# One mixture-of-experts layer: slot gates in the PSUM copy, and adding DMA loads onto the residual rows

## The chip, the core and the metric

The kernel runs on one core of one Trainium2 chip. The metric is the device time of one execution in microseconds (us). A profile of one execution gives the trace that is read here; its times count from the first instruction.

## What is computed

One layer of a streaming encoder over 512 tokens of width 1024, in float32. Two mixers (an SSD scan and an HGRN2 scan) and an output projection give the residual rows `x`. Behind them comes a mixture of 16 experts in 4 groups: each token takes its best group and in it the best two experts.

```python
p_group = jax.nn.softmax(t @ router_group);  g_idx = argmax(p_group);  g_w = max(p_group)
top_w, top_i = lax.top_k(jax.nn.softmax(in_group), 2)       # in_group: the group's 4 logits
top_w = top_w / jnp.sum(top_w)
combine = sum(one_hot(expert_id, 16) * (g_w * top_w))       # per token, 2 of 16 are not zero
hid = silu(t @ wg) * (t @ wu)                               # per expert, 256 wide
x = x + sum over experts of combine * (hid @ wd)
return rmsnorm(x, final_norm_w)
```

So each token ends as its residual row plus two expert rows, each times a gate, and then a norm.

## The kernel before

Every engine has its own instruction stream, written by hand; semaphores order them. The span has four parts: input projections and mixers (to about 255 us), output projection with the routers' logits (to 283), routing (283 to 298), experts (298 to 450), and a tail (450 to the end).

**Routing.** DVE turns the logits into one-hot choices and slots. `onehot` maps tokens to up to 112 slots of an expert. PE multiplies `onehot` with small tables (`find_all`, `find_targets`): `gix` says which token sits in a slot, `six` to which output row a slot's result goes. `keep_warm(n)` issues n matmuls whose result nobody reads. GpSimd (POOL) then gathers the token rows of experts 0 to 3 from `h2_dram` (L667), DVE works off the leftovers of routing (L1479 to L1494, the last of them counting rounds), splits expert weights into a high and a low part (`split_b` L1506, `split_c` L1512) and does the same to the gathered tokens (`rest_tokens` L1500) once PE has turned them (`turn_tokens` L1962) and ACT has copied them (L975). SP loads 3 MB of weights per expert, in the order in which splits free the buffers.

**Experts.** For each of 16 experts PE forms gate, up and down products, ACT copies the two halves of the output out of PSUM into `ysb` (L1008, L1010), and POOL scatters its 112 rows into `pairs_dram` (L688). That tensor has two halves of 512 rows: the row of the token's expert with the lower place in its group is in the first, the other's in the second. All rows of the first half are written once 12 of the 16 experts are done.

**Tail.** SP loads the first half in four loads of 0.5 MB (`load_early`, L544) after expert 13's work has been handed out, and DVE computes the gates (`gates`) and adds each loaded row times its gate to the residual row (L1570). SP loads the second half when all scatters have landed (L572). For each of four tiles of 128 tokens DVE adds (L1596), ACT sums squares and takes the root (L1036, L738), DVE norms (L1602), SP stores (L575).

**Later rounds.** If an expert has more than 112 tokens, everything from `find_all` on is repeated; each engine reads the number of rounds into a register (L443) and branches (L444) past the repeated code. With these inputs nothing is repeated. In the kernel before this stands ahead of the tail.

Of the kernel before, what the change touches and what calls it, by code (L numbers as in the profile page):

```python
# [5 lines left out]
ALU = mybir.AluOpType  # L6
# [37 lines left out]
def trunk(nc, x, norm_mix_w, w_units, w_dt, conv_w, conv_b, dt_bias, a_log, d_skip, ssd_norm_w, hgrn_lb_logits,  # L44
# [97 lines left out]
    with ExitStack() as ctx:  # L142
# [101 lines left out]
        onehot = gate[:, 0, :].bitcast(F16).rearrange("p (c t s) -> p c t s", c=2, t=TT)  # L244
        vals = part(TT * NE).bitcast(F16).rearrange("p (c t e) -> p c t e", c=2, t=TT)
# [11 lines left out]
        wcol = part(KD)  # L257
        rtw = part(KD * NL).rearrange("p (k n) -> p k n", k=KD)
        ss = part(TT * D // UC).rearrange("p (t u) -> p t u", t=TT)
# [13 lines left out]
        early = [raw[:, 1, 0:D], raw[:, 1, D:2 * D], arena[:, 0:D], arena[:, D:2 * D]]  # L273
        late = [arena[:, a:a + D] for a in range(8 * D, 12 * D, D)]
# [141 lines left out]
        res_ok = sem("res_ok")  # L416
# [9 lines left out]
        early_ok = sem("early_ok")  # L426
# [4 lines left out]
        h2_dram = nc.dram_tensor("h2_dram", (T, HROW), F32, kind="Internal").ap()  # L431
        pairs_dram = nc.dram_tensor("pairs_dram", (2 * T, D), F32, kind="Internal").ap()
# [7 lines left out]
        def later_rounds(eng, body):  # L440

            eng.wait_ge(routed, 1)
            n = eng.value_load(rounds[0:1, 0:1], min_val=1, max_val=MOST)  # L443
            with eng.If(n > 1):  # L444
                with eng.Fori(1, n) as r:
                    body(r, r * NE)
            return n
# [28 lines left out]
        def _(sp):  # L476
# [42 lines left out]
            def sp_round(r, base, first_round=False):  # L519
                for e in range(WSETS if first_round else 0, NE + 1):  # L520
# [9 lines left out]
                    if e < NE:  # L530
                        if e == 0:
                            sp.wait_ge(early_ok, r * TT)
                        else:
                            sp.wait_ge(wlb_ok, (base + max(e - WSETS + 1, 0)) * 2)
                        load_b(e)

            def load_early(rows_done, first_round=False):
                for j in range(YB):
                    sp.wait_ge(sca_out[j], rows_done)
                if first_round:  # L540
                    wait_a(sp, 0, NE - 2)
                    sp.wait_ge(wlb_ok, (NE - 2) * 2)
                for tt in range(TT):
                    sp.dma_start(early[tt], pairs_dram[tt * P:(tt + 1) * P, :]).then_inc(early_in, 16)  # L544

            def sp_later(r, base):
                sp_round(r, base)
                load_early(r * (16 * PER_Y) + 16 * PER_Y)
# [12 lines left out]
            load_c(2)  # L561
            sp.wait_ge(gat_in[0], 16)
# [4 lines left out]
            load_early((NE - G) // YB * 16, True)  # L567
            n = later_rounds(sp, sp_later)
            for j in range(YB):
# [3 lines left out]
            for tt in range(TT):  # L573
                sp.wait_ge(fin_ok, tt + 1)
                sp.dma_start(out[0, tt * P:(tt + 1) * P, :], late[tt]).then_inc(out_st, 16)  # L575
            sp.wait_ge(out_st, 16 * TT)

        @block.gpsimd
        def _(pool):
# [101 lines left out]
            def scatter(r, base, e):  # L681
# [3 lines left out]
                if e == 0:  # L685
                    pool.wait_ge(six_ok, r + 1)
# [3 lines left out]
                    .then_inc(sca_out[j], 16)  # L690

            def pool_round(r, base, first_round=False):
# [9 lines left out]
                for e in range(NE):  # L702
# [4 lines left out]
                    scatter(r, base, e)  # L707

# [5 lines left out]
            later_rounds(pool, pool_round)  # L714
# [10 lines left out]
        def _(act):  # L725
# [260 lines left out]
            def act_expert(r, base, e, first_round):  # L986
# [15 lines left out]
                if e + 2 < NE:  # L1002
                    round_b(r, e + 2)
                elif e + 1 < NE:
                    round_hidden(step + 1, e + 1)
                act.wait_ge(dn, step * 2 + 3)
                y_free(act, r, e, first_round)
                sc.activation(ysb[e % YB][:, 0:512], bank[5][:, :], ACT.Copy).then_inc(y0_ok, 1)  # L1008
                act.wait_ge(dn, step * 2 + 4)
                sc.activation(ysb[e % YB][:, 512:1024], bank[6][:, :], ACT.Copy).then_inc(y1_ok, 1)  # L1010
# [20 lines left out]
            later_rounds(act, act_round)  # L1031

            ch.link(sc.activation(dec[:, 0, 0:1], ident[:, 0:1], ACT.Sqrt))
            for tt in range(TT):
                act.wait_ge(res_ok, tt + 1)
                ch.link(sc.activation(X[:, tt, :], late[tt], ACT.Square, accum_out=st[:, 0, tt:tt + 1]))  # L1036
                root(st[:, 5, tt:tt + 1], st[:, 0, tt:tt + 1], 1.0 / D).then_inc(fsd_ok, 1)

        @block.vector
        def _(dve):  # L1040
# [427 lines left out]
            def targets(r):  # L1468

                dve.wait_ge(six_mm, r + 1)  # L1470
                ve.tensor_scalar(six, bank[7][:, NE:2 * NE], float(NO_SLOT), None, ALU.add).then_inc(six_ok, 1)
# [19 lines left out]
            for k in range(2, MOST):  # L1491
                ch.link(ve.scalar_tensor_tensor(rnd[:, 1:2], rnd[:, 0:1], float(k * CAP), rnd[:, 1:2], ALU.is_gt,
                                                ALU.add))
            ve.tensor_copy(rounds, rnd[:, 1:2]).then_inc(routed, 1)  # L1494
# [44 lines left out]
            def dve_round(r, base, first_round=False):  # L1539
# [543 lines left out]
```

## Time and profile before

| | us |
|---|---|
| median of 3 runs (lowest, highest) | 476.56 (475.51, 476.58) |
| the profiled execution, its own time | 476.44 |
| its span, first to last instruction | 474.7 |
| PE busy (share of the span) | 434.1 (91%) |
| DVE busy | 341.3 (72%) |
| ACT busy | 272.5 (57%) |
| POOL busy | 155.3 (33%) |

A view of the trace lists instructions with start, length, engine, source line, operation and, in brackets, how long the engine sat idle before and who released it. The chain of waits follows the work that ended last backwards. Engine time off that chain costs nothing. The timeline's length of a transfer issued by POOL is the time that POOL takes to issue it, not that of the data.

### The profile page before, as it was taken

To read this page: it belongs to the slowest core of one execution; us is meant where nothing else is said; L and a number is where in the kernel's file an instruction comes from. 1 tells how busy PE (TensorE), PEld (TensorE's weight loads), DVE (VectorE), ACT (ScalarE), POOL (GpSimd) and SP (SyncE) were. 2 spreads that over 40 slices of the span, in tenths; PEclk is the share of its full clock that TensorE was granted. 3 is DMA by queue.
4 is the path that set the end of the run, shared out by engine and by line. 5 is a ranking of instruction groups with operands and counts; after the bars stand their busy time and mean duration, and the time that the engine had idled before them with its cause. 6 is when DMAs were issued, how large, how long until landed. Compare 5 with 4: busy or idle time off the path is not lost.

```text
span 474.7 us, 7158 instructions
## 1 busy us (share of the span) xinstructions
PE 434.1 (91%) x2785; PEld 382.3 (81%) x2785; DVE 341.3 (72%) x523; ACT 272.5 (57%) x444; POOL 155.3 (33%) x114
## 2 busy tenths in 40 slices
PE   6999999999999899999999996999999999999800
PEld 4888888899998699899999986888888888887500
DVE  5535887783769689899866258677887787758836
ACT  6654182623543343228254335598998999879523
POOL 5620000000005000212400403388878887865210
PEclk9999999999999999999999998999999999999955
DMA  8632222222204002224199602989999999987264
GB/s 314 245 111 90 89 90 88 90 88 90 90 1 139 40 1 90 88 96 171 51 370 307 258 18 60 321 306 363 384 384 350 375 385 373 359 336 290 79 212 198
DMA packets 20626, 92.47 MB, mean 195 GB/s; under 512 B 4797, under 2 KB 7017, under 8 KB 12138
## 3 DMA queue, kind: packets, MB, share of 16 engines
q1 hardware_dynamic: 13848, 81.42, 45.9%
q0 software_dynamic: 4096, 8.41, 5.3%
q10 hardware_dynamic: 2642, 2.11, 1.4%
q8 instruction: 24, 0.39, 0.4%
q14 instruction: 16, 0.13, 0.1%
HBM read 86.69 MB, written 11.54 MB: 207 GB/s over the span
## 4 chain that ended last, share of the span: by engine, by line
PE 69%; DVE 14%; DMA 9%; ACT 6%; issue 2%; SPq 0%; POOLq 0%; DVEq 0%; ACTq 0%
PE bank L1641 41%; DMA arena<-in_w_gate_up_dram 5%; PE bank L1974 4%; PE bank L1976 4%; PE bank L1975 4%; PE bank L1962 2%; PE bank L1839 1%; DVE wl L1506 1%; DMA X<-in_x_dram 1%; DMA pairs_dram<-arena 1%; DVE actl L1052 1%; DVE actl L1512 1%; DMA X<-h_dram,arena 1%; PE bank L1711 1%; DVE arena L1602 1%
## 5 line engine op out<-in xcount | busy, mean ns | idle before, releaser
L1641 PE MATMUL bank<-wh,acth 128*128 128x256 f32 x320 | 91.8, 287 | 1.4 <-DVE actl L1052 0.8
L1641 PE MATMUL bank<-wl,acth 128*128 128x256 f32 x320 | 90.5, 283 | 0.0
L1641 PE MATMUL bank<-wh,actl 128*128 128x256 f32 x320 | 90.4, 283 | 0.0
L618 POOL TENSOR_TENSOR wl<-raw,wh 128x2048 fp32r<-128x2048 f32 x4 | 20.5, 5137 | 134.4 <-ACT wh L734 134.4
L1641 PEld LDWEIGHTS bank<-wh,acth 128*128 128x128 f32 x320 | 61.2, 191 | 1.8 <-issue 1.7
L1641 PEld LDWEIGHTS bank<-wl,acth 128*128 128x128 f32 x320 | 61.3, 192 | 0.0
L1641 PEld LDWEIGHTS bank<-wh,actl 128*128 128x128 f32 x320 | 61.2, 191 | 0.0
L1974 PE MATMUL bank<-wh,acth 128*128 128x512 f32 x128 | 51.7, 404 | 0.9 <-DVE wl L1506 0.7
L1976 PE MATMUL bank<-wh,actl 128*128 128x512 f32 x128 | 50.1, 392 | 0.0
L1975 PE MATMUL bank<-wl,acth 128*128 128x512 f32 x128 | 49.9, 390 | 0.0
L678 POOL TENSOR_TENSOR wl<-raw,wh 128x1024 fp32r<-128x1024 f32 x15 | 36.0, 2421 | 42.0 <-ACT wh L923 42.0
L1641 PE MATMUL bank<-acth,wh 128*128 128x512 f32 x112 | 44.1, 394 | 0.1
L1641 PE MATMUL bank<-acth,wl 128*128 128x512 f32 x112 | 43.6, 390 | 0.0
L1641 PE MATMUL bank<-actl,wh 128*128 128x512 f32 x112 | 43.6, 389 | 0.0
L678 POOL TENSOR_TENSOR wl<-arena,wh 128x1024 fp32r<-128x1024 f32 x16 | 39.0, 2463 | 13.0 <-ACT wh L923 13.0
L734 ACT ACTIVATE wh<-raw 128x2048 fp32r<-128x2048 f32 x18 | 34.4, 1909 | 15.4 <-PE bank L1641 15.4
L1512 DVE TENSOR_TENSOR actl<-arena,acth 128x1024 fp32r<-128x1024 f32 x30 | 35.9, 1234 | 1.3 <-ACT acth L937 1.0
L1058 DVE TENSOR_TENSOR wl<-raw,wh 128x2048 fp32r<-128x2048 f32 x14 | 32.0, 2288 | 3.5 <-ACT wh L734 3.4
L1500 DVE TENSOR_TENSOR actl<-bank,acth 128x512 fp32r<-128x512 f32 x32 | 20.6, 686 | 17.7 <-ACT acth L975 17.7
L1506 DVE TENSOR_TENSOR wl<-arena,wh 128x1024 fp32r<-128x1024 f32 x20 | 27.0, 1391 | 7.7 <-ACT wh L928 7.7
L937 ACT ACTIVATE acth<-arena 128x1024 fp32r<-128x1024 f32 x30 | 30.0, 1055 | 0.0
L1974 PEld LDWEIGHTS bank<-wh,acth 128*128 128x128 f32 x128 | 24.0, 188 | 6.7 <-issue 1.9
(349 smaller groups left out, 1016.8 us busy)
## 6 DMA issues: line engine op xcount, KB each, us to landing
raw<-in_w_units_dram SPq DMA_DIRECT2D x18, 1024.0 KB, 4.9
arena<-in_w_gate_up_dram SPq DMA_DIRECT2D x18, 1024.0 KB, 16.4
arena<-in_w_down_dram SPq DMA_DIRECT2D x16, 1024.0 KB
raw<-in_w_gate_up_dram SPq DMA_DIRECT2D x14, 1024.0 KB, 15.1
arena<-pairs_dram SPq DMA_DIRECT2D x6, 512.0 KB, 5.4
X<-in_x_dram SPq DMA_DIRECT2D x4, 512.0 KB, 5.2
arena<-in_x_dram SPq DMA_DIRECT2D x1, 2048.0 KB, 9.9
h_dram<-X ACTq DMA_DIRECT2D x4, 512.0 KB, 4.7
```

The costliest lines, as they stand in the source:

```text
L618: gp.tensor_tensor(wl[:, u % SPL, :], raw[:, u % RAW, :], wh[:, u % SPL, :].bitcast(F32), ALU.subtract).then_inc(wlp_ok, 1)
L678: gp.tensor_tensor(wl[:, 0, c], raw_a[b][:, c], wh[:, 0, c].bitcast(F32), ALU.subtract).then_inc(wla_ok, 1)
L734: sc.activation(wh[:, u % SPL, :], raw[:, u % RAW, :], ACT.Copy).then_inc(wh_ok, 1)
L937: sc.activation(down_high(e)[:, c], raw_c[e % WSETS][:, c], ACT.Copy).then_inc(whc_ok, 1)
L1058: ve.tensor_tensor(wl[:, u % SPL, :], raw[:, u % RAW, :], wh[:, u % SPL, :].bitcast(F32), ALU.subtract).then_inc(wl_ok, 1)
L1500: ve.tensor_tensor(gtl[b][:, c], bank[2 + h][:, :], gth[b][:, c].bitcast(F32), ALU.subtract).then_inc(gl_ok, 1)
L1506: ve.tensor_tensor(wl[:, 1, c], raw_b[e % WSETS][:, c], wh[:, 1, c].bitcast(F32), ALU.subtract).then_inc(wlb_ok, 1)
L1512: ve.tensor_tensor(down_low(e)[:, c], raw_c[e % WSETS][:, c], down_high(e)[:, c].bitcast(F32), ALU.subtract).then_inc(wlc_ok, 1)
L1641: ins = te.matmul(acc_ap, a, b, start=(j == 0), stop=(j == n - 1))
L1974: te.matmul(bank[b][:, :], ah, uh[:, k, :], start=(first and k == 0), stop=False)
L1975: te.matmul(bank[b][:, :], ah, ul[:, k, :], start=False, stop=False)
L1976: ins = te.matmul(bank[b][:, :], al_, uh[:, k, :], start=False, stop=(last and k == kh - 1))
```

## The change

1. **Gates move into routing.** The gates' arithmetic goes from behind the last expert to just behind `vals6`. A table of the gate values, as a sum of three bfloat16 parts (`gvp`), is multiplied with the same one-hot matrix on PE in 24 more small matmuls (`find_targets`), and gives `gsl`, one gate per slot and expert. The `keep_warm(4)` behind `find_targets` goes. Counting the rounds moves behind `split_c`, and `rest_tokens(0)` moves ahead of it.
2. **The gate is applied in the copy out of PSUM**, as the scale of the two ACT copies per expert.
3. **The additions are done by DMA.** `add_early` and `add_late`, issued by POOL, load rows of `pairs_dram` with `accum_op=add` onto the residual rows `xres`. DVE's eight additions of a tile and SP's eight loads go. `add_early` stands in POOL's stream behind the scatter of expert 13, `add_late` behind the last scatter; it waits until all scatters and the early additions have landed.
4. **The residual rows are kept** in `xres_dram` by two stores on SP (`keep_rows`, 1.5 and 0.5 MB), since later rounds would start again from them.
5. **The read of the number of rounds and the branch** come behind the tail: the tail is always done, and again if there were later rounds. On SP they stand behind the wait for the output stores.

```diff
+            def store_out(k):
+                for tt in range(TT):
+                    sp.wait_ge(fin_ok, k * TT + tt + 1)
+                    sp.dma_start(out[0, tt * P:(tt + 1) * P, :], xres[:, tt, :]).then_inc(out_st, 16)
+                sp.wait_ge(out_st, (k + 1) * 16 * TT)
...
+            sp.wait_ge(ev_dve, evacuated(n_in_groups + halves_out.index((n_front - 2, 1)))[1])
+            keep_rows(slice(0, units[n_front - 1][1]))
+            sp.wait_ge(h2_st, 16 * (n_front - n_in + 1))
+            keep_rows(slice(units[n_front - 1][1], D))
             sp.wait_ge(gat_in[0], 16)
             load_a(3)
...
-            load_early((NE - G) // YB * 16, True)
-            n = later_rounds(sp, sp_later)
-            for j in range(YB):
-                sp.wait_ge(sca_out[j], n * (16 * PER_Y))
-            for tt in range(TT):
-                sp.dma_start(late[tt], pairs_dram[T + tt * P:T + (tt + 1) * P, :]).then_inc(late_in[tt], 16)
...
+            store_out(0)
+            later_rounds(sp, sp_round, rows_again, lambda n: store_out(1))
...
+            def add_early(k):
+                pool.sem_inc(pool_tick, 1)
+                for tt in range(TT):
+                    gp.dma_start(xres[:, tt, :], pairs_dram[tt * P:(tt + 1) * P, :],
+                                 accum_op=ALU.add).then_inc(early_in, 16)
+
+            def add_late(k):
+                pool.wait_ge(early_in, (k + 1) * 16 * TT)
+                pool.sem_inc(pool_tick, 1)
+                for tt in range(TT):
+                    gp.dma_start(xres[:, tt, :], pairs_dram[T + tt * P:T + (tt + 1) * P, :],
+                                 accum_op=ALU.add).then_inc(late_in[tt], 16)
...
+                weight = gsl[:, PERM[e]:PERM[e] + 1]
+                sc.activation(ysb[e % YB][:, 0:512], bank[5][:, :], ACT.Copy, scale=weight).then_inc(y0_ok, 1)
...
+            gv = r16[:, 4:6]
+            ch.link(ve.tensor_tensor(gv, r16[:, 1:3], r1[:, 8:10].unsqueeze(3).broadcast_to([P, 2, TT, NE]), ALU.mult))
+            for i in range(2):
+                ch.link(ve.tensor_copy(gvp[:, i], gv))
+                ch.link(ve.tensor_tensor(gv, gv, gvp[:, i], ALU.subtract))
+            ve.tensor_copy(gvp[:, 2], gv).then_inc(gt_v, 1)
...
                 split_b(base, 0, 0)
                 split_b(base, 0, 1)
+                rest_tokens(base, 0)
                 split_c(base, 0, 0)
-                rest_tokens(base, 0)
                 split_c(base, 0, 1)
+                if first_round:
+                    count_rounds()
...
+                pe.wait_ge(gt_v, 1)
+                for c in range(2):
+                    for tt in range(TT):
+                        for i in range(3):
+                            ins = te.matmul(bank[7][:, 2 * NE:3 * NE], onehot_b[:, c, tt, :], gvp[:, i, c, tt],
...
                 keep_warm(8)
                 find_targets(r)
-                keep_warm(4)
                 turn_tokens(r, base, 0)
```

DVE at the end of routing, where `CAST arena<-arena 128x128` makes a part of the gate table. Before:

```order
L1488 TENSOR_TENSOR arena<-arena 128x64 x2
L1492 SCALAR_TENSOR_TENSOR arena<-arena 128x1 x3
L1494 CAST arena<-arena 128x1
L1506 TENSOR_TENSOR wl<-raw,wh 128x1024 x2
L1512 TENSOR_TENSOR actl<-arena,acth 128x1024
L1500 TENSOR_TENSOR actl<-bank,acth 128x512 x2
L1512 TENSOR_TENSOR actl<-arena,acth 128x1024
```

and in the changed kernel:

```order
L1522 TENSOR_TENSOR arena<-arena 128x64 x2
L1526 TENSOR_REDUCE arena<-arena 128x4
L1528 SCALAR_TENSOR_TENSOR arena<-arena 128x4
L1529 RECIPROCAL arena<-arena 128x4
L1530 TENSOR_TENSOR arena<-arena 128x4
L1533 TENSOR_TENSOR arena<-arena 128x128
L1535 CAST arena<-arena 128x128
L1536 TENSOR_TENSOR arena<-arena 128x128
L1535 CAST arena<-arena 128x128
L1536 TENSOR_TENSOR arena<-arena 128x128
L1537 CAST arena<-arena 128x128
L1555 TENSOR_TENSOR wl<-raw,wh 128x1024 x2
```

Ten operations come ahead of the first weight split, four leave that place; `rest_tokens` (L1549 in the changed kernel) follows the split at once.

POOL from the scatter of expert 13 to the branch. Before:

```order
L678 TENSOR_TENSOR wl<-arena,wh 128x1024 x2
L688 DMA pairs_dram<-arena 1024x1024 x3
L443 TENSOR_LOAD arena
L443 ISA x2
L444 COMPARE_AND_BRANCH
```

and in the changed kernel:

```order
L677 TENSOR_TENSOR wl<-arena,wh 128x1024 x2
L687 DMA pairs_dram<-arena 1024x1024
L694 DMA arena<-pairs_dram 128x1024 x4
L687 DMA pairs_dram<-arena 1024x1024 x2
L701 DMA arena<-pairs_dram 128x1024 x4
L447 TENSOR_LOAD arena
```

Four loads stand between the scatters of experts 13 and 14, four behind that of expert 15.

SP behind its last weight load. Before:

```order
L566 DMA bc<-in_final_norm_w_dram 128x1024
L544 DMA raw<-pairs_dram 128x1024 x2
L544 DMA arena<-pairs_dram 128x1024 x2
L443 TENSOR_LOAD arena
L443 ISA x2
L444 COMPARE_AND_BRANCH
```

and in the changed kernel:

```order
L573 DMA bc<-in_final_norm_w_dram 128x1024
L547 DMA out_dram<-arena 128x1024 x4
L447 TENSOR_LOAD arena
L447 ISA x2
L448 COMPARE_AND_BRANCH
```

The eight loads of `pairs_dram` are gone from SP, and the value load with its branch stands behind the output stores.

## Rows read from the trace of the kernel before

**Rows 1.** The chain that ended last, from 449 us: start, length, what.

```profile
449.93 0.61 ACT arena L1010
...
451.38 5.36 DMA pairs_dram<-arena
...
456.82 3.51 DMA arena<-pairs_dram
```

**Rows 2.** The timeline of the tail: start, length, engine, line, operation [idle before].

```profile
451.38 1.35 POOL L688 DMA_INDIRECT pairs_dram<-arena  x1 [1.04 <-ACT arena L1010]
...
460.45 2.48 DVE L1596 SCALAR_TENSOR_TENSOR arena<-arena,raw 128x1024 f32<-128x1024 f32 x2 [7.34 <-DMA arena<-pairs_dram]
...
468.65 1.06 ACT L1036 ACTIVATE X<-arena 128x1024 f32<-128x1024 f32 x1 [1.11 <-DVE arena L1596]
...
470.17 0.16 DVE L1601 RECIPROCAL st<-st 128x1 f32<-128x1 f32 x1 [0.15 <-ACT st L738]
470.36 1.28 DVE L1602 SCALAR_TENSOR_TENSOR arena<-arena,st,bc 128x1024 f32<-128x1024 f32 x1
```

**Rows 3.** Source line L142, the end of the block.

```profile
L142 SPq COMPARE_BRANCH  x1: 38/38/38, 474.3 to 474.3; - x1
```

**Rows 4.** Transfers on pairs_dram from 420 us to the end.

```profile
L572 SPq DMA_DIRECT2D arena<-pairs_dram x4: 323/424/432, 456.8 to 458.1; - x4
...
DMA to landing us min/median/max: 3.5/5.4/7.2
```

**Rows 5.** A window of 2 us in the late loads; last columns DMA share, GB/s.

```profile
460.00:462.00 2.00, 0.00 (x0) 0.00 (x0) 1.54 (x2) 0.16 (x1) 0.00 (x0) 0.50 0.99 383
```

**Rows 6.** The timeline of POOL from 425 us.

```profile
430.58 0.96 POOL L688 DMA_INDIRECT pairs_dram<-arena  x1 [3.93 <-ACT arena L1010]
...
438.83 1.91 POOL L688 DMA_INDIRECT pairs_dram<-arena  x1 [1.12 <-ACT arena L1010]
448.58 1.76 POOL L688 DMA_INDIRECT pairs_dram<-arena  x1 [7.84 <-ACT arena L1010]
```

**Rows 7.** The timeline of POOL at the first gathers.

```profile
291.55 1.23 POOL L667 DMA_INDIRECT X<-h_dram,arena  x1 [4.30 <-DVE arena L1466]
293.08 1.87 POOL L667 DMA_INDIRECT X<-h_dram,arena  x1 [0.31 <-issue]
```

**Rows 8.** Source line L443, the value load ahead of the later rounds.

```profile
L443 SPq TENSOR_LOAD <-arena x1: 478/478/478, 430.1 to 430.1; - x1
```

**Rows 9.** Source line L444, the branch past the later rounds.

```profile
L444 DVEq COMPARE_BRANCH  x1: 72/72/72, 449.2 to 449.2; - x1
```

**Rows 10.** Source line L570, what SP does behind its branch.

```profile
L570 SPq ALU_OP  x1: 48/48/48, 431.1 to 431.1; - x1
```

**Rows 11.** Source line L1591, what DVE does behind its branch.

```profile
L1591 DVEq ALU_OP  x1: 57/57/57, 452.0 to 452.0; - x1
```

**Rows 12.** The timeline of DVE at the end of routing.

```profile
288.31 0.29 DVE L1454 TENSOR_REDUCE arena<-arena 128x8 f32<-128x128 f32 x1
...
291.89 0.54 DVE L1492 SCALAR_TENSOR_TENSOR arena<-arena 128x1 f32<-128x1 f32 x3
...
292.86 2.36 DVE L1506 TENSOR_TENSOR wl<-raw,wh 128x1024 fp32r<-128x1024 f32 x2 [0.24 <-issue]
...
297.16 1.29 DVE L1500 TENSOR_TENSOR actl<-bank,acth 128x512 fp32r<-128x512 f32 x2 [0.81 <-ACT acth L975]
```

**Rows 13.** The timeline of PE at the end of routing.

```profile
293.06 0.35 PE L1952 MATMUL bank<-arena,gate 128*128 128x16 f16 x8
...
295.84 1.09 PE L1962 MATMUL bank<-ident,X 128*128 128x128 f32 x8 [1.43 <-DMA X<-h_dram,arena]
```

**Rows 14.** Windows around the expert stage; last columns PEclk, DMA share, GB/s.

```profile
340.00:380.00 40.00, 40.00 (x197) 33.41 (x197) 31.88 (x35) 36.67 (x53) 32.79 (x18) 1.00 0.99 373
436.00:448.00 12.00, 10.73 (x48) 8.10 (x47) 10.73 (x18) 7.98 (x13) 3.62 (x2) 1.00 0.33 130
270.00:278.00 8.00, 8.00 (x70) 7.99 (x69) 2.90 (x6) 1.84 (x7) 2.11 (x1) 1.00 0.01 3
```

More of the change, by code:

```diff
@@ L257, in trunk @@
         wcol = part(KD)
+        gvp0 = ofs[0]
         rtw = part(KD * NL).rearrange("p (k n) -> p k n", k=KD)
+        part(3 * TT * NE - KD * NL)
+        gvp = arena[:, gvp0:gvp0 + 3 * TT * NE].bitcast(BF16).rearrange("p (i c t e) -> p i c t e", i=3, c=2, t=TT)
+        gsl = part(NE)
         ss = part(TT * D // UC).rearrange("p (t u) -> p t u", t=TT)
@@ L271, in trunk @@
         rounds = part(1).bitcast(I32)
-        early = [raw[:, 1, 0:D], raw[:, 1, D:2 * D], arena[:, 0:D], arena[:, D:2 * D]]
-        late = [arena[:, a:a + D] for a in range(8 * D, 12 * D, D)]
         assert ofs[0] <= 22528
@@ L438, in trunk, with later_rounds @@
         PER_Y = NE // YB
-        def later_rounds(eng, body):
+        def later_rounds(eng, body, before=None, after=None):
             eng.wait_ge(routed, 1)
@@ L444, in later_rounds @@
             with eng.If(n > 1):
+                if before is not None:
+                    before()
                 with eng.Fori(1, n) as r:
                     body(r, r * NE)
-            return n
+                if after is not None:
+                    after(n)
         def set_uses(r, e, sets):
@@ L690, in scatter, with add_again @@
                     .then_inc(sca_out[j], 16)
+            def add_early(k):
[9 more added lines that the diff above has]
+                                 accum_op=ALU.add).then_inc(late_in[tt], 16)
+            def add_again(n):
+                for j in range(YB):
+                    pool.wait_ge(sca_out[j], n * (16 * PER_Y))
+                pool.wait_ge(xres_in, 32)
+                add_early(1)
+                add_late(1)
             def pool_round(r, base, first_round=False):
@@ L707, in pool_round @@
                     scatter(r, base, e)
+                    if first_round and e == NE - 3:
+                        for j in range(YB):
+                            pool.wait_ge(sca_out[j], (NE - G) // YB * 16)
+                        pool.wait_ge(xr_st, 32)
+                        add_early(0)
             split_a(0, 0)
@@ L713, in _ @@
             pool_round(0, 0, True)
-            later_rounds(pool, pool_round)
+            for j in range(YB):
+                pool.wait_ge(sca_out[j], 16 * PER_Y)
+            add_late(0)
+            later_rounds(pool, pool_round, None, add_again)
         def conv_at(jj):
@@ L1030, in _, with final_sums @@
             act_round(0, 0, True)
[L1031 to L1037, printed above, removed]
+            def final_sums(k):
+                ch.link(sc.activation(dec[:, 0, 0:1], ident[:, 0:1], ACT.Sqrt))
+                for tt in range(TT):
+                    act.wait_ge(late_in[tt], (k + 1) * 16)
+                    ch.link(sc.activation(X[:, tt, :], xres[:, tt, :], ACT.Square, accum_out=st[:, 0, tt:tt + 1]))
+                    root(st[:, 5, tt:tt + 1], st[:, 0, tt:tt + 1], 1.0 / D).then_inc(fsd_ok, 1)
+            final_sums(0)
+            later_rounds(act, act_round, None, lambda n: final_sums(1))
         @block.vector
```

101 lines of the change are left out of this document (37 added, 64 removed).

## The prediction

> **What bounds the kernel now.** I read the chain of waits first, then the timeline of its last 25 us, then the places that the change touches. Up to 450 us the chain is PE and the weights' DMA, and in the expert stage the DMA engines are as good as full: a share of 0.99 at 373 GB/s from 340 to 380 us [rows 14]. Behind the last PSUM copy, which ends at 449.93 + 0.61 = 450.54, everything is a chain of handovers [rows 1]: the last scatter from its issue at 451.38 to its landing 5.36 us later (456.74), the first late load 3.51 us (456.82 to 460.33), and then tile work. That work is paced by DVE, which has an addition and a norm of 1.28 us for each tile, and its last norm ends at 470.36 + 1.28 = 471.64 [rows 2]. The last store has landed when SP goes on at 474.3 [rows 3]. So 24 of the 474.7 us are tail, and most of the change is there.
>
> **The tail, step by step, in times of this trace.**
>
> 1. *Last scatter.* Its issue took POOL 1.35 us [rows 2], and one took 0.96 us where DVE was less in the way [rows 6]. In the changed kernel DVE has no additions there, so I take 0.96: it lands 0.39 earlier, at 456.35. The start, 0.84 us behind the copy's end (450.54 to 451.38), stays.
>
> 2. *POOL answers instead of SP.* SP issued 0.08 us after the landing (456.74 to 456.82); POOL needs 0.84 as above. First adding load: issue at 456.35 + 0.84 = 457.19.
>
> 3. *First adding load, if it were a plain one.* On SP: 3.51 us from issue, of which 0.32 are SP's own issue (the shortest of four) [rows 4], so 3.19 behind it. On POOL with 0.96 of issue: 457.19 + 0.96 + 3.19 = 461.34.
>
> 4. *Pace.* Plain loads of 0.5 MB ran at 383 GB/s with the engines at a share of 0.99 [rows 5], which makes 1.37 us for each. An adding load has to fetch the old row as well as the new one before it can write. The trace of before has no such load. From below it costs what a plain one does, 1.37; the other end is two transfers' worth, 2.74, since engines at 0.99 have no time left for a second fetch. I take 2.74 for this reason. Then the first lands at 461.34 + 1.37 = 462.71 and the fourth 3 x 2.74 = 8.22 later, at 470.93. POOL's issues (four of about 1.3 us with their gaps) are faster than that.
>
> The Trainium skill, "Collectives: The Full Stack", in the section "The bandwidth ceiling: the fold count and why AG ≠ RS ≠ AR", says that a transfer which reduces runs at about half the speed of a copy because it reads two sources, not because the addition takes time. It speaks of collectives and no run here shows it yet; by it the pace is the 2.74 of step 4, and without it the sum would be that of the first rival. It is the rule that speaks most against this change.
>
> 5. *From the fourth landing to the end.* DVE began 0.12 after a landing (460.33 to 460.45); ACT now takes its place. From the start of the last square (468.65) to the end of the last norm (471.64) are 2.99, and from there to the landed store at 474.3 are 2.66 [rows 2, 3]. 470.93 + 0.12 + 2.99 + 2.66 = 476.70. DVE's addition is gone here, but at this pace it would have been hidden for all tiles except the last.
>
> 6. *Value load and branch on SP* stood at 430 us behind the early loads, under a long wait; now they stand behind the wait for the stores, where nothing covers them. From the value load at 430.1 to SP's next instruction behind the branch at 431.1 is 1.0 us [rows 8, 10]. 477.7, and the end of the block another 0.4 (474.3 to 474.7 as before): 478.1, so +3.4 against the span of 474.7. On the other engines the same pieces lie under the stores: DVE's takes 0.9 + 2.8 us from its load on, but it starts as soon as the last norm is issued.
>
> 7. *Early adding loads ahead of the last scatters.* POOL is free at 438.83 + 1.91 = 440.74 [rows 6] and starts 0.3 later. Its issue beside busy DVE costs up to 1.9 each [rows 7], so four end by 449.9 at the latest, against 448.58, when the scatter of expert 14 is issued; with 0.96 at its best they end at 446. That is covered within about 1 us. The data is the larger matter: first landing at 441.05 + 0.96 + 3.19 + 1.37 = 446.6, the fourth at 454.8, its data moved some 1.8 earlier (3.19 - 1.37), at 453.0. The two last scatters are issued by the same engine into the same queue; if they line up behind, their 2 x 0.46 MB need at least 2 x 1.2 us at 383 GB/s and 1.8 to land: 457.2, or 458 if they don't run at full speed, against 456.35. I take +1.4. Bounds: 0 (they pass by) to 3.
>
> Sum: +3.4 + 1.4 = +4.8, against the profiled execution's own 476.44 (span 474.7 and 1.7 around it): **481.2**. The median of the runs shown, 476.56, is 0.1 from it, so nothing is shifted.
>
> **What costs nothing, and its cover.** *DVE in routing:* behind the target table (at about 291.9) come four operations on 4 elements, some 0.2 each, and six on 128 elements, 0.29 for the like [rows 12] and 0.03 between: 0.8 + 1.9 = 2.7, to 294.6, where 1.0 stood before. The split starts at 294.6 instead of 292.86, takes 2.36 and ends at 297.0; the next on the path, `rest_tokens`, started at 297.16 because it waited for ACT [rows 12], and that waited for the gathered rows. So the cover is 0.2 us; it holds only because `split_c` moves behind. What is late next is SP's second and third load (1 us later), behind a first one of 1 MB, which at 373 GB/s [rows 14] is 2.8 us of data. *PE:* 24 matmuls at 0.35 for 8 [rows 13] are 1.05, from 294.6 to 295.7, and the turning of the first gathered rows behind them began at 295.84: cover 0.1 us. If both covers fail, routing slips by 0.3 to 1 us, of which the full DMA engines of the expert stage take back a part. *Keeping the rows:* 1.5 MB go where the DMA share is 0.01 (270 to 278) [rows 14], 0.5 MB behind the last store of token rows and ahead of the gathers, whose first is issued at 291.55 [rows 7]. *Scale in the PSUM copy:* same instruction, none added; ACT's new wait for the gate table stands before its first such copy, which needs all products of expert 0 first. *Gates, early additions and early loads* taken away: DVE sat idle for 7.34 us before the first late addition [rows 2], and the DMA share behind 436 was 0.33 [rows 14]. Nothing gained.
>
> **The rivals.**
>
> *A, on the other side: the adding loads run like plain ones.* Then the fourth lands at 461.34 + 3 x 1.37 = 465.45, and DVE, with a norm and a reciprocal for each tile (0.16 + 1.28 and gaps, 1.48) instead of an addition more, sets the end: the first norm starts at 461.34 + 0.12 + 1.71 = 463.17 (468.65 to 470.36 is the 1.71), the last ends 3 x 1.48 + 1.28 later at 468.9, store 2.66, SP 1.0, end 0.4: 473.0, so -1.7 and **474.7**. For it: the engines may fetch from SBUF beside DRAM. Against it: their share of 0.99. It decides at 4x = 7.56, a pace x of 1.9 us for each 0.5 MB: slower than that is a loss.
>
> *B, nothing to measure.* As A, but SP's branch costs what DVE's does, which is 2.8 us from the branch at 449.2 to the next instruction at 452.0 [rows 9, 11], not 0.1: +1.8 on A, **476.5**. Or a pace near 1.9. Against it: SP's own branch over nearly the same code was short. The Trainium skill, "Runtime: NRT & Kernel Launch", section "Instruction fetch mechanics", says that a taken branch to code outside the loaded window stalls for a fetch; by that rule SP's tail would be 2.8 longer whenever its code has moved across such a border, and the two rows here show both cases.
>
> *C, much slower.* If an adding load's fetch, fetch and write follow one another for each row, the pace is 3 x 1.37 = 4.11: fourth landing at 464.1 + 12.3 = 476.4, +8.9, and the early loads hold the last scatters back by some 7 us: **492**. Nothing in the trace speaks for or against it but that the operation is new.
>
> **How the numbers follow.** The forecast 0.55, A 0.22, B 0.12, C 0.11. A measurement of this kernel can tell some 0.3% (1.4 us) from no change. A is faster with nearly all its chance, B is same, forecast and C are slower: 0.23, 0.13, 0.64. The forecast's own range is 478.5 (no scatter held back, pace 2.4) to 484 (scatters 3 late, routing 1 late). For 8 in 10 I reach down to A and up to a pace of about 3: 474.5 to 486, which leaves out C and the edge of A.
>
> **What the next profile would show.** Right: loads issued by POOL behind the last scatter, landing 2.5 to 3 us apart; ACT's squares waiting for each of them; about 1 us between SP's last wait and the end. Wrong: squares or norms back to back with no wait for a landing (A); a gap of 3 us behind SP's branch (B); scatters of experts 14 and 15 that land as before in spite of slow early loads (step 7); `rest_tokens` later than 297.2, or the granted clock down behind 293 (routing).

## The result, and the profile after

The changed kernel takes 480.73 us (median of 4, 479.93 to 484.35), the kernel before beside it 476.46 (4 runs, 475.51 to 476.58). The ratio is 1.0112 with an interval of 1.0068 to 1.0156: slower, by 0.7 to 1.6%. The profiled execution took 479.94, its span is 478.2.

I read the chain of waits first, as for before. From the end of the last PSUM copy on it shows start, length, what:

```profile
449.23 0.70 ACT arena L1040
...
450.79 6.01 DMA pairs_dram<-arena
...
457.37 1.71 POOL arena L701 x2
459.07 11.71 DMA arena<-pairs_dram
470.79 0.02 issue
470.81 1.16 ACT X L1066 x2
...
472.52 1.28 DVE arena L1627
```

The last copy ends at 449.92, 0.6 earlier than before [rows 1], and the last scatter lands at 456.80, where it landed at 456.74: up to here nothing is lost. Then one piece of 11.71 us stands where 3.51 stood [rows 1]: the last adding load. The timeline of the same stretch shows who waits for it:

```profile
457.37 3.67 POOL L701 DMA_DIRECT2D arena<-pairs_dram  x4 [5.60 <-DMA pairs_dram<-arena]
463.07 1.06 ACT L1066 ACTIVATE X<-arena 128x1024 f32<-128x1024 f32 x1 [11.65 <-DMA arena<-pairs_dram]
...
465.51 1.06 ACT L1066 ACTIVATE X<-arena 128x1024 f32<-128x1024 f32 x1 [0.96 <-DMA arena<-pairs_dram]
...
467.99 1.06 ACT L1066 ACTIVATE X<-arena 128x1024 f32<-128x1024 f32 x1 [1.00 <-DMA arena<-pairs_dram]
...
470.81 1.06 ACT L1066 ACTIVATE X<-arena 128x1024 f32<-128x1024 f32 x1 [1.34 <-DMA arena<-pairs_dram]
```

Each of the four squares has an idle time ahead of it that a load ended, so the DMA sets the pace, where DVE did before [rows 2]. The landings (462.99, 465.49, 467.97, 470.79) are 2.60 us apart on average. The windows show the engines full, and the data at a little over half its rate (last columns DMA share, GB/s):

```profile
444.00:452.00 8.00, 5.05 (x22) 3.41 (x20) 0.92 (x3) 4.51 (x7) 1.99 (x2) 1.00 1.07 208
462.00:470.00 8.00, 0.00 (x0) 0.00 (x0) 3.37 (x6) 4.33 (x9) 0.00 (x0) 0.50 1.06 215
```

The first line is the early adding loads (with packets of the last two scatters among them), the second the late ones; plain loads had 383 GB/s at 0.99 [rows 5]. The end of the program, by source line, is SP's value load behind the wait for the stores and the branch behind it, whose rows had stood at 430 and 431 [rows 8, 10]:

```profile
L447 SPq TENSOR_LOAD <-arena x1: 462/462/462, 477.0 to 477.0; - x1
```

```profile
L448 SPq COMPARE_BRANCH  x1: 45/45/45, 477.8 to 477.8; - x1
```

The stores have landed at 476.98 and the span ends at 478.20. Routing, in the timeline of DVE (first fence) and PE (second), to be held against [rows 12, 13]:

```profile
294.65 0.23 DVE L1537 CAST arena<-arena 128x128 bf16<-128x128 f32 x1
295.04 2.39 DVE L1555 TENSOR_TENSOR wl<-raw,wh 128x1024 fp32r<-128x1024 f32 x2 [0.16 <-issue]
298.57 1.29 DVE L1549 TENSOR_TENSOR actl<-bank,acth 128x512 fp32r<-128x512 f32 x2 [1.15 <-ACT acth L1002]
```

```profile
294.94 0.76 PE L1980 MATMUL bank<-arena,gate 128*128 128x16 bf16 x24 [2.08 <-DVE arena L1537]
296.34 1.66 PE L1991 MATMUL bank<-ident,X 128*128 128x128 f32 x8 [0.64 <-issue]
...
299.35 0.77 PE L2003 MATMUL bank<-wh,acth 128*128 128x512 f32 x1
```

PE stands idle for 2.08 us until the gate table is there, and turns the tokens at 296.34 instead of 295.84; `rest_tokens` starts 1.41 later than before, and still waits for ACT.

**How tails are compared.** When the last PSUM copy ends varies by some 2 us each way between executions (449.9 to 454.2 in the profiles of this study). What follows it doesn't vary so: "the tail" below is the time from the end of that copy to the end of the span. Two profiles of one kernel on two chips gave 23.49 and 23.48 (the last experiment); single terms inside a tail differ more than that. Before it is 474.68 - 450.53 = 24.2, after it 478.20 - 449.92 = 28.3. So the tail lost 4.1 us, and the measured ratio stands for 0.0112 x 476.46 = 5.3 us (3.2 to 7.4); the medians differ by 4.3.

### The profile page after: what moved, and what is told of

The parts are those of the page before. It is cut to its first block, busy times and chain, and to the rows that moved or that the text cites. A ratio compares the mean times of both kernels' runs of the same rounds, so it can differ in the third digit from the quotient of the medians.

```text
span 478.2 us, 7184 instructions
## 1 busy us (share of the span) xinstructions
PE 434.9 (91%) x2801; PEld 383.8 (80%) x2801; DVE 333.6 (70%) x516; ACT 275.7 (58%) x444; POOL 159.5 (33%) x122
## 4 chain that ended last, share of the span: by engine, by line
PE 77%; DVE 11%; DMA 5%; ACT 5%; issue 1%; POOL 0%; SPq 0%; POOLq 0%; DVEq 0%
PE bank L1663 43%; PE bank L2003 6%; PE bank L2005 6%; PE bank L2004 6%; PE bank L1991 3%; DMA arena<-pairs_dram 2%; PE bank L1861 1%; DMA pairs_dram<-arena 1%; DMA X<-in_x_dram 1%; DVE actl L1085 1%; PE bank L1733 1%; PE bank L1734 1%; PE bank L1741 1%; PE bank L2028 1%; ACT arena L781 1%
## 5 line engine op out<-in xcount | busy, mean ns | idle before, releaser
L1663 PEld LDWEIGHTS bank<-wh,acth 128*128 128x128 f32 x320 | 61.3, 192 | 1.2 <-issue 1.0
L1663 PEld LDWEIGHTS bank<-wh,actl 128*128 128x128 f32 x320 | 61.3, 191 | 0.0
L1549 DVE TENSOR_TENSOR actl<-bank,acth 128x512 fp32r<-128x512 f32 x32 | 20.6, 686 | 16.8 <-ACT acth L1002 16.8
L1555 DVE TENSOR_TENSOR wl<-arena,wh 128x1024 fp32r<-128x1024 f32 x20 | 28.8, 1480 | 4.2 <-ACT wh L955 4.2
L2005 PEld LDWEIGHTS bank<-wh,actl 128*128 128x128 f32 x128 | 24.1, 188 | 5.3
```

The costliest lines, as they stand in the source:

```text
L1549: ve.tensor_tensor(gtl[b][:, c], bank[2 + h][:, :], gth[b][:, c].bitcast(F32), ALU.subtract).then_inc(gl_ok, 1)
L1555: ve.tensor_tensor(wl[:, 1, c], raw_b[e % WSETS][:, c], wh[:, 1, c].bitcast(F32), ALU.subtract).then_inc(wlb_ok, 1)
L1663: ins = te.matmul(acc_ap, a, b, start=(j == 0), stop=(j == n - 1))
L2005: ins = te.matmul(bank[b][:, :], al_, uh[:, k, :], start=False, stop=(last and k == kh - 1))
```

## The experiments

The theory was the prediction's: the tail is longer because an adding load costs the DMA engines two transfers, the branch adds 1 us, the early adding loads hold the last scatters back, and the move of the gates costs nothing. The rivals were that the loss lies in routing, that it comes from how POOL issues such a load, or from its rows.

**Gates in routing alone.** The kernel before with part 1 and 2 of the change: SP loads, DVE adds (now without a gate), the branch is ahead of the tail.

```diff
-                    ve.scalar_tensor_tensor(early[tt], early[tt], r1[:, 10, tt:tt + 1], xres[:, tt, :], ALU.mult,
-                                            ALU.add).then_inc(early_ok, 1)
+                    ve.tensor_tensor(early[tt], early[tt], xres[:, tt, :], ALU.add).then_inc(early_ok, 1)
```

> The kernel before with the gates made in routing and applied in the PSUM copies, but with SP's plain loads and DVE's additions as before (now without a factor), no stored residual rows and the branch ahead of the tail. Theory (the adding loads are the loss): no change against before, 476.5 within 1 us, since the routing slip of about 1.4 us in the changed kernel was gone again at the end of the experts. Rival (the routing slip reaches the end): 478, and the last PSUM copy ends 1 us or more later than at 450.5.

Measured: 476.14 (12 runs, 474.28 to 479.03), ratio 1.0003 (0.9978 to 1.0028), tail 23.5. Half of the change costs nothing and gains nothing that can be measured, though its profiled tail is 0.7 shorter than before's 24.2, and though routing is late in this kernel too: from the first gather to the first product of the experts it takes 298.68 - 290.87 = 7.8 us, before 297.91 - 291.55 = 6.4.

**Late loads plain.** The changed kernel with the four late loads on POOL, where they were, but without the addition. It leaves out what `xres` held, the residual and the first rows.

```diff
-                    gp.dma_start(xres[:, tt, :], pairs_dram[T + tt * P:T + (tt + 1) * P, :],
-                                 accum_op=ALU.add).then_inc(late_in[tt], 16)
+                    gp.dma_start(xres[:, tt, :],
+                                 pairs_dram[T + tt * P:T + (tt + 1) * P, :]).then_inc(late_in[tt], 16)
```

> The changed kernel with the four late loads plain instead of adding, still issued by POOL; this leaves the other expert's row and the residual row out of the result. Theory (two fetches for each adding load): the landings stand 1.3 to 1.5 us apart instead of 2.5 to 2.8, DVE's norms set the end, and the time falls by about 5 us, to 475. Rival (the software queue or POOL's issue sets the pace, not the addition): landings stay 2.5 apart and the time stays at 480.

Measured: 476.98 (12 runs, 474.65 to 480.02), ratio 1.0018 (0.9990 to 1.0046), tail 24.2: 4.1 less than with the addition, which is as much as the tail had lost. The chain of waits of this kernel:

```profile
454.06 6.07 DMA pairs_dram<-arena
...
460.70 1.11 POOL arena L701 x2
461.81 6.54 DMA arena<-pairs_dram
468.35 0.02 issue
468.37 1.16 ACT X L1066 x2
```

The landings are 464.32, 465.63, 468.35 and 469.61, so 1.31, 2.72 and 1.26 apart. The third came 1.4 late. Stores of finished tiles are not the reason: the first was issued at 467.49, and without the delay the third load would have landed at 466.9. The kernel before shows the same step: its plain loads landed at 460.33, 461.61, 464.07 and 465.34, and its first store was issued at 464.86. The windows around its third landing (last columns DMA share, GB/s):

```profile
463.00:464.00 1.00, 0.00 (x0) 0.00 (x0) 0.61 (x2) 0.98 (x2) 0.00 (x0) 0.50 0.40 160
464.00:465.00 1.00, 0.00 (x0) 0.00 (x0) 1.00 (x2) 0.65 (x3) 0.00 (x0) 0.50 0.06 25
```

A share of 0.06 is one engine of 16. The trace has 16 reports of each load, one from each engine, and the landing is the last of them. Of that third load 15 reports came from 462.39 to 462.90 and the last at 464.07: one engine was 1.2 us late. In the kernel with plain late loads it was several (12 reports by 467.05, the others from 467.64 to 468.35). Why is open. So plain loads of 0.5 MB land 1.67 us apart on average in the kernel before, and 1.76 here, though most engines keep a pace of about 1.3.

**Two adding, two plain.** The first two late loads add, the other two don't. It leaves out the residual and first rows of tiles 2 and 3.

```diff
-                for tt in range(TT):
+                for tt in range(2):
                     gp.dma_start(xres[:, tt, :], pairs_dram[T + tt * P:T + (tt + 1) * P, :],
                                  accum_op=ALU.add).then_inc(late_in[tt], 16)
+                for tt in range(2, TT):
+                    gp.dma_start(xres[:, tt, :],
+                                 pairs_dram[T + tt * P:T + (tt + 1) * P, :]).then_inc(late_in[tt], 16)
```

> The changed kernel with late adding loads for the first two tiles and plain ones for the last two; this leaves the other summands out of tiles 2 and 3. Theory: two landings about 2.6 apart and two about 1.3 to 2, so the fourth landing comes 1.5 to 2.5 us earlier than in the changed kernel counted from the first issue (13.4 there), and the tail from the last PSUM copy to the end shrinks by as much, from 28.3 to about 26. Rival (a fixed price for using adding loads at all): no earlier than with four.

Measured: 479.81 (12 runs, 477.95 to 481.61), ratio 1.0073 (1.0043 to 1.0104), tail 26.1, in the middle between 24.2 and 28.3. Landings 465.98, 468.52, 469.80, 471.07: 2.54 apart for the second adding load, 1.28 and 1.27 for the plain ones. One kernel, one queue, one execution, and the windows in each half (last columns DMA share, GB/s):

```profile
463.00:468.00 5.00, 0.00 (x0) 0.00 (x0) 0.32 (x2) 1.44 (x3) 0.35 (x1) 0.50 1.05 208
469.00:471.00 2.00, 0.00 (x0) 0.00 (x0) 1.04 (x3) 1.97 (x5) 0.00 (x0) 0.50 1.03 420
```

The engines are full in both; in the first the adding loads move 208 GB/s, in the second the plain ones 420 (stores of finished tiles counted).

**Short rows.** The late adding loads of a tile in two halves of 512 columns, so with rows of 2 KB.

```diff
-                    gp.dma_start(xres[:, tt, :], pairs_dram[T + tt * P:T + (tt + 1) * P, :],
-                                 accum_op=ALU.add).then_inc(late_in[tt], 16)
+                    for c in (slice(0, D // 2), slice(D // 2, D)):
+                        gp.dma_start(xres[:, tt, c], pairs_dram[T + tt * P:T + (tt + 1) * P, c],
+                                     accum_op=ALU.add).then_inc(late_in[tt], 16)
```

> The changed kernel with each late adding load cut into two of 512 columns, so rows of 2 KB instead of 4 KB, same bytes. Theory (each byte is fetched twice): a tile still lands every 2.5 to 2.8 us, its packets take half as long as the 4 KB ones (about 150 ns instead of 300), time within 1 us of the changed kernel's. Rival (each row pays a fetch, add and write in turn, whatever its length): twice the rows, so a tile every 4 to 5 us and 485 to 490.

Measured: 484.20 (4 runs, 482.01 to 485.78), ratio 1.0160 (1.0092 to 1.0228), tail 30.8. The squares of the four tiles:

```profile
465.66 1.06 ACT L1067 ACTIVATE X<-arena 128x1024 f32<-128x1024 f32 x1 [11.92 <-DMA arena<-pairs_dram]
...
469.15 1.06 ACT L1067 ACTIVATE X<-arena 128x1024 f32<-128x1024 f32 x1 [2.01 <-DMA arena<-pairs_dram]
...
471.82 1.06 ACT L1067 ACTIVATE X<-arena 128x1024 f32<-128x1024 f32 x1 [1.20 <-DMA arena<-pairs_dram]
...
475.73 1.06 ACT L1067 ACTIVATE X<-arena 128x1024 f32<-128x1024 f32 x1 [2.43 <-DMA arena<-pairs_dram]
```

3.38 us for each 0.5 MB. Neither side's number came out. The records of single packets tell more: the median adding packet of 2 KB took 178 ns, one of 4 KB in the changed kernel 328, a plain one of 4 KB in the kernel with plain late loads 159. So an adding packet costs by its bytes, at 4 KB twice a plain one, with about 28 ns beside that (2 x 178 - 328, an estimate from the two sizes). Of 0.5 MB each of the 16 engines moves 8 packets of 4 KB: 8 x 328 ns = 2.62 us, the pace seen with adding loads, and 8 x 159 = 1.27, which is the pace of plain ones where no engine is late. With 2 KB it is 16 x 178 = 2.85. The other 0.5 us of the 3.38 have a likely source in the queue rows. Here the stores of finished tiles (q1) run among the late loads, from 465.57 to 475.71:

```profile
q0 software_dynamic: 783, 1.41, 80.9%
q1 hardware_dynamic: 264, 1.00, 24.7%
```

That is 2.5 us of every engine. In the changed kernel, between its first and fourth landing, the same queue took 13.2% of 7.80 us, so 1.0. The difference is 1.5 us for three spacings, or 0.5 for each, as much as was missing. It was not tested by itself.

**No early adding loads.** It leaves out the first expert rows.

```diff
-                        add_early(0)
...
-                pool.wait_ge(early_in, (k + 1) * 16 * TT)
```

> The changed kernel without the four early adding loads; this leaves the first expert's rows out of the result. Prediction's step 7: the last scatter's data lined up behind them, so its landing, 6.01 us behind its issue, comes back to 5.4 or less and the time falls by 0.5 to 1.4 us. Rival: the landing stays and so does the time.

Measured: 481.68 (4 runs, 479.10 to 483.36), ratio 1.0102 (1.0049 to 1.0154), tail 27.4, 0.9 shorter than after. The time doesn't show it: 0.9 us is 0.2% and lies inside the interval of 4 runs. The chain of waits does:

```profile
455.40 4.16 DMA pairs_dram<-arena
```

The last scatter needs 4.16 us from issue to landing, and 6.01 behind early adding loads; in the five other profiles with such loads it needed 5.79 to 6.15. Against the kernel before, where it took 5.36, the loss is smaller: 0.65. Of the 1.85 some 0.3 each are lost again ahead of the scatter, until the fourth landing and behind it.

**No later rounds.** The value load and the branch are taken away on all engines (these inputs need one round).

```diff
-            later_rounds(sp, sp_round, rows_again, lambda n: store_out(1))
```

> The changed kernel without the reading of the number of rounds, the branch and the repeated code on all engines; this leaves out later rounds, of which these inputs need none. Theory: SP's value load and branch lie bare behind the stores, so the time falls by 1.0 us, to about 479. Rival (a fetch behind the branch): by 2.8 us. Other rival (hidden): by nothing.

Measured: 480.53 (4 runs, 478.58 to 482.06), ratio 1.0101 (1.0047 to 1.0155), tail 26.6, 1.7 shorter than after. The end of the block on SP:

```profile
L142 SPq COMPARE_BRANCH  x1: 33/33/33, 477.2 to 477.2; - x1
```

The span ends at 477.58, 0.4 behind the landed stores; after it ends 1.2 behind them. So 0.8 us are the value load and the branch on SP. The other 0.9 of the shorter tail lie ahead of that: the last scatter lands 0.2 sooner, the four loads take 0.1 less, and the last store lands 2.65 us behind the last norm instead of 3.18. The first two are no more than what a single term varies by. The third is not chance. In all six profiled kernels whose branch stands behind the tail this store took 3.0 to 3.6 us from its issue, and in the six others, this one among them, 2.6. In the six with the longer store ACT and DVE branch 0.2 to 1.1 us before it is issued, in the changed kernel ahead of 473.83:

```profile
L448 ACTq COMPARE_BRANCH  x1: 50/50/50, 473.2 to 473.2; - x1
L448 DVEq COMPARE_BRANCH  x1: 72/72/72, 473.5 to 473.5; - x1
```

Behind these, from 473 to the end of the span, the instruction queue (q14) uses the DMA engines, which it does in none of the six others:

```profile
q14 instruction: 4, 0.03, 2.4%
```

Its four packets of 8 KB hold an engine for 0.3 to 0.6 us each, and of the changed kernel's last store 15 parts were reported by 476.54, the last at 476.98. That the loading of code is what holds that part back is argued, not tested. With it the branch's new place costs about 1.3 us instead of 0.8. The times don't show any of this: by the ratios this kernel is 0.5 us faster than the changed one, inside the noise.

**Warm matmuls back.** `keep_warm(4)` between the product of the targets and the wait for the gate table.

```diff
+                keep_warm(4)
                 pe.wait_ge(gt_v, 1)
```

> The changed kernel with the four warming matmuls put back, between the target product and the wait for the gate table. Theory of routing: TensorE's granted clock no longer falls to half around 296 us, and the first gate and up product starts about 1 us earlier than at 299.4; the time falls by 0 to 1 us, since the full DMA engines of the expert stage decide. Rival (the slip goes through): by the whole 1 to 1.4 us.

Measured: 480.98 (6 runs, 479.58 to 483.01), ratio 1.0106 (1.0053 to 1.0158), tail 28.4. In the changed kernel the granted clock is at its lower level, 1.2 of 2.4 GHz, for 3.4 us from 296.7, with PE idle for 2.08 us shortly before; here that drop is missing (one of 3.4 us stands at 289.7) and the turning takes 1.09 us again:

```profile
297.17 1.09 PE L1992 MATMUL bank<-ident,X 128*128 128x128 f32 x8 [1.04 <-DMA X<-h_dram,arena]
```

But it waits for the gathered rows, and the experts start no earlier: 299.74, 7.3 us behind the first gather, as in the changed kernel. Nothing is gained: the clock was not what made routing late. That the drop is missing needn't be the work of the four matmuls either: it is missing in the next experiment too, which doesn't have them.

**POOL adds the last tile.** The kernel of the first experiment, with the last late addition on POOL.

```diff
+            pool.wait_ge(res_ok, 1)
+            pool.wait_ge(late_in[TT - 1], 16)
+            gp.tensor_tensor(late[TT - 1], late[TT - 1], early[TT - 1], ALU.add).then_inc(res3_ok, 1)
```

> The kernel of the first experiment (gates applied in the PSUM copies, plain loads) with the last tile's addition done by POOL instead of DVE. DVE sets the end of the tail there with an addition and a norm of 1.28 us for each tile, POOL adds in about 2.5 us what landed at 465.9: theory, the tail from the last PSUM copy shrinks by 0.3 to 1.0 us from 23.5, the time by as much, too little to be sure of. Rival (the two engines hold each other up): longer.

Measured: 476.54 (12 runs, 474.73 to 478.12), ratio 1.0008 (0.9978 to 1.0037), tail 23.7. The timeline of DVE, and that of POOL:

```profile
466.45 3.18 DVE L1615 SCALAR_TENSOR_TENSOR arena<-arena,st,bc 128x1024 f32<-128x1024 f32 x1
```

```profile
465.48 3.06 POOL L724 TENSOR_TENSOR arena<-arena 128x1024 f32<-128x1024 f32 x1 [11.88 <-DMA arena<-pairs_dram]
```

A norm that takes 1.28 alone takes 3.18 beside POOL's addition: it gives back what DVE was spared.

**One adding load.** The same kernel with the last tile's late rows added by one adding load, where DVE might hide it.

```diff
-            for tt in range(TT):
+            for tt in range(TT - 1):
                 sp.dma_start(late[tt], pairs_dram[T + tt * P:T + (tt + 1) * P, :]).then_inc(late_in[tt], 16)
...
+            gp.dma_start(early[TT - 1], pairs_dram[2 * T - P:2 * T, :],
+                         accum_op=ALU.add).then_inc(late_in[TT - 1], 16)
```

> The kernel of e1 (gates in routing, plain loads by SP, additions by DVE), but the last of the four late tiles is added by one adding load that POOL issues; DVE adds three tiles and norms four. POOL's two waits ahead of it are written for one round, which is what these inputs need. Theory (an adding load costs two transfers' worth of the DMA engines and nothing else, so one of them is hidden where DVE sets the pace): the engines have 3 x 1.3 + 2.6 = 6.5 us of late data, the last landing is about 9 us behind the last scatter's, and in e1 DVE began its last addition 10 us behind it. So the adding load is hidden, DVE has one operation of 1.22 us less, and the tail from the end of the last PSUM copy to the end of the span is 22.4 us where e1 had 23.5; the ratio to before is 0.998, within 0.3% of no change. Rival (the adding load takes its share from the plain ones from the first moment, so that the first two landings are late by up to 1.3 us each): DVE's first additions start later and the tail is 23.5 us or more.

Measured: 477.09 (12 runs, 472.44 to 480.39), ratio 1.0014 (0.9986 to 1.0042), tail 24.6: the rival's side. The profiled execution was the longest of the twelve (480.39), so the reading of its tail is weaker than the others. DVE's additions:

```profile
463.29 1.23 DVE L1616 TENSOR_TENSOR arena<-arena,raw 128x1024 f32<-128x1024 f32 x1 [8.70 <-DMA arena<-pairs_dram]
...
464.91 1.23 DVE L1616 TENSOR_TENSOR arena<-arena,raw 128x1024 f32<-128x1024 f32 x1 [0.40 <-DMA arena<-pairs_dram]
...
469.94 1.22 DVE L1616 TENSOR_TENSOR arena<-arena 128x1024 f32<-128x1024 f32 x1 [2.34 <-DMA arena<-pairs_dram]
```

The third plain load landed at 469.92, 5.0 us behind the second (464.89), and it was a plain load that DVE waited for. In the four profiles of kernels with SP's plain loads alone that spacing is 2.0 to 2.8. Of the 5.0 us, 2.4 are one engine: 15 of the load's 16 parts were reported by 467.48. So that the adding load slows the plain ones is likely, but its size isn't shown, nor that the late engine is its work, since one is late in the kernel before too. My theory counted full engines throughout; a window from 462 to 470 shows a share of 0.97, one from 460 to 463 only 0.63. On the same chip the kernel without the adding load had a ratio of 0.9982 (below), which agrees in sign, but the two intervals overlap.

**The first kernel again.** Unchanged, to see how a tail varies.

> The kernel of e1 once more, unchanged, on the chip of e9, so that the two can be compared and that it is seen how much its tail varies between profiled executions. Theory: ratio to before 0.998 to 1.003, tail from the last PSUM copy to the end of the span within 0.4 us of 23.5. Rival: tails vary between executions by 1 us and more, as the time of the last PSUM copy does, and then the differences of 0.8 and 0.9 us read from the tails of e3 and e4 are not settled.

Measured: 475.36 (12 runs, 473.76 to 478.16), ratio 0.9982 (0.9958 to 1.0006), tail 23.5 as the first time. Of the gates alone there are now 24 runs on two chips, with ratios 1.0003 and 0.9982. No version tried beats both kernels by what can be measured; the gates' move comes nearest.

## Why the prediction was right

Forecast 481.2, measured 480.73 as the median and 479.94 in the profile. The forecast case held, not a rival. The total is nearer than its terms, whose errors of up to 0.5 us have both signs. Its tail by terms, worked out from the times in its steps, against the trace (us):

| step | predicted | measured |
|---|---|---|
| last copy's end to the issue of the last scatter | 0.84 | 0.87 |
| 1 and 7, that scatter to its landing | 6.37 | 6.01 |
| 2, POOL answers | 0.84 | 0.57 |
| 3, first adding load, issue to landing | 5.52 | 5.62 |
| 4, three further landings | 8.22 | 7.80 |
| 5, to the end of the last norm | 3.11 | 3.01 |
| 5, from there to the landed stores | 2.66 | 3.18 |
| 6, value load, branch, end of the block | 1.40 | 1.22 |
| tail | 28.96 | 28.28 |

*Step 4 is the one that decides, and it is shown.* The pace is 2.60 us where 2.74 was taken, and the addition alone, put in or left out, moves the tail by 4.1 us and the ratio from 1.0018 to 1.0112. With two of four loads adding half of it comes back. Rival A (1.37 us) and C (4.11) are out. The step's 1.37 us is what plain loads need by their rate; their landings in the trace of before are 1.67 apart on average, since one engine was late. The adding loads had no engine that late (the reports of each load lie within 0.9 us), so twice the rate's figure fitted them. The rule of the Trainium skill, "Collectives: The Full Stack", section "The bandwidth ceiling: the fold count and why AG ≠ RS ≠ AR", which speaks of collectives, gives the right rate here for a DMA load: this case's trace agrees, 208 GB/s against 420 within one execution. That the second source is the reason, as the rule has it, no run here shows by itself.

*Step 7 is shown by the landing time, not by the ratio.* The last scatter took 4.16 us without early adding loads and 6.01 with them, so in these two profiles they hold it back by 1.85. I took 1.4, but on top of 4.97 us (5.36 less the shorter issue), where 4.16 was measured without them: the hold-up was taken too short and the rest too long, and that their sum is only 0.36 off is in part luck. Its issue took 0.98 as taken in step 1 (0.96).

*Step 6 is shown for SP:* 0.8 us for the value load and the branch; 1.0 was taken. Rival B needed a fetch of 2.8 us behind SP's branch, as in the rule of the Trainium skill, "Runtime: NRT & Kernel Launch", section "Instruction fetch mechanics", on a taken branch out of the loaded window; 0.4 us behind the branch at 477.8 the span was over, so on SP it did not come. B's own sum was off besides: 2.8 us in place of 0.1 are 2.7 on top of A, so 477.4 and not 476.5.

*Step 5 was short by 0.5 us.* I took the last store's 2.66 from a kernel in which the stores before it had more time. Here it was 3.18, in the kernel with plain late loads 3.4, and without the rounds' code 2.65 again. Step 6 had counted the other engines' branches as hidden under the stores; the code that is loaded behind them stands beside the longer store in all six kernels that have it, as the experiment without later rounds shows. So this term probably belongs to the branch's new place.

*The two covers failed, as the text had allowed.* The gate table was there at 294.88 and the split at 295.04 (294.6 predicted for both), PE stood idle for 2.08 us ahead of its product with the gate table, and the first product of the experts is 1.44 later than before. Of these 0.46 are the first gather's, which came later already (292.01 against 291.55 [rows 7]); in the profiles of the ten experiments that gather lies between 290.87 and 292.52. So the slip is 1.0, the upper end of 0.3 to 1, and from the first gather to the first product it is 7.2 to 7.8 us in every kernel with the gates in routing, against 6.4 before. It was taken back: the last PSUM copy ends 0.6 us earlier than before. That the slip costs nothing is shown by the gates alone (1.0003 and 0.9982). That the full DMA engines of the expert stage (a share of 0.98 from 340 to 380, as in [rows 14]) are what takes it back is an argument and was not tested.

**Where the gain went that the change could have brought:** DVE's additions are gone from the tail, and with plain late loads and all the rest of the change the tail is 24.2, no shorter than before. POOL's answer (0.5 more than SP's), the scatter held back, the branch (0.8) and the longer last store (0.7 in that kernel) are about the size of what DVE is spared; the slow loads then put 4.1 us on top.

## What to carry to other kernels

An adding DMA load takes the time of two transfers on the DMA engines: use it where their share is low and nobody waits for it, and not in a tail in which they are full already; it also holds back what is queued behind it. A branch that is moved behind the tail may cost something on the other engines too, if they load code beside the last stores. Work that is spared on an engine is worth only what the next wait leaves of it, so price the replacement at the place where it stands. To tell 1 us in 480, compare the stretch behind a fixed event (here the last PSUM copy) and not the whole time, which varied by 5 us between executions.

## What the runs showed that I had not expected

- An adding packet of 4 KB took 328 ns, a plain one 159; of 2 KB 178. Rows of half the length cost more in sum, 3.38 us for 0.5 MB against 2.60, of which 0.5 are probably stores that run beside them.
- A load waits for the slowest of 16 engines: the third of four plain loads landed 2.46 us behind the second in the kernel before and 5.0 in the one with an adding load beside it, and one engine made 1.2 and 2.4 of that.
- The last store took 2.6 us where no code was loaded beside it and 3.0 to 3.6 where it was.
- POOL's issue of a plain load of 0.5 MB took 0.56 us and of an adding one 0.95 to 1.96, each longer than the one before, with starts 0.6 apart either way; two plain ones behind two adding ones took 1.25.
- The granted clock falls to its lower level for 3.4 us at places that differ between kernels and executions (from 283.7 to 297.4 us, and near 164 in some). Once it stayed there for 6.8 us, and in the gates-only kernel once for 10.2 from 288.4; the ratio of that kernel was still 1.0003.
